# Norm hand-overs between layers, token half by token half, with the first two matmul units of each later norm laid tokens-on-partitions

## The reference

```python
for l in range(2):                                   # layers 0 and 1
    h = rmsnorm(x, g[0])
    y = even_mixer(h, ...) if l == 0 else odd_mixer(h, ...)
    x = x + rmsnorm(y, g[1])
    h = rmsnorm(x, g[2])
    x = x + rmsnorm(square(relu(h @ w1)) @ w2, g[3])
# then one hybrid layer:
h = rmsnorm_2(x, norm_g) * (1 + scale) + shift
proj = h @ w_in      # q, k, v, gates, convolution inputs
...
return rmsnorm_2(x + gate * (merged @ w_out), final_g)
```

## Time and profile before

| | us |
|---|---|
| median of 3 runs | 1006.33 |
| lowest and highest | 1002.78, 1007.84 |
| the profiled execution | 1001.67 |
| its span in the trace | 999.8 |
| PE busy | 972.2 (97%) |
| DVE busy | 646.5 (65%) |
| ACT busy | 503.0 (50%) |

### The profile page before, as it was taken

The page is one execution under the profiler, slowest core; times in us unless marked ns, Lnnn a source line. Parts: engine busy times, 40 slices in busy tenths (PEclk is TensorE's granted clock), DMA queues, the critical chain, the costliest instruction groups (busy, mean ns, idle before and its releaser), DMA issues.

```text
span 999.8 us, 14613 instructions
## 1 busy us (share of the span) xinstructions
PE 972.2 (97%) x6122; PEld 881.9 (88%) x6122; DVE 646.5 (65%) x821; ACT 503.0 (50%) x588; POOL 14.0 (1%) x12
## 2 busy tenths in 40 slices
PE   6999999999999999999999999998999999999997
PEld 5998888799999988888799999987989999988885
DVE  5889936567666658856567666657443777646473
ACT  6734464545444446565645444446444555435433
POOL 0000000000000000000000000000000000002000
PEclk9999999999999999999999999999999999999999
DMA  9834426457777773444457777791756445557511
GB/s 316 298 127 130 165 87 208 147 169 252 253 234 231 239 219 123 166 167 126 148 169 252 252 235 232 247 245 64 263 172 206 157 141 168 169 174 247 191 62 42
DMA packets 124900, 187.37 MB, mean 187 GB/s; under 512 B 5315, under 2 KB 92836, under 8 KB 124836
## 3 DMA queue, kind: packets, MB, share of 16 engines
q1 hardware_dynamic: 124676, 186.17, 57.3%
q10 hardware_dynamic: 160, 0.27, 0.1%
HBM read 185.37 MB, written 1.06 MB: 186 GB/s over the span
## 4 chain that ended last, share of the span: by engine, by line
PE 93%; DVE 4%; issue 1%; DMA 1%; ACT 1%; SPq 0%; DVEq 0%; ACTq 0%
PE bank L568 91%; DVE wl L982 1%; DVE scr L982 1%; DMA raw<-in_ev_w_in 1%; PE bank L724 1%; DVE arena L982 1%; PE bank L795 0%; DVE x L988 0%; DVE hl L988 0%; ACT wh L1515 0%; PE bank L869 0%; ACT arena L1510 0%; PE bank L683 0%; ACT hh L1510 0%; DVE work L985 0%
## 5 line engine op out<-in xcount | busy, mean ns | idle before, releaser
L982 DVE TENSOR_TENSOR wl<-raw,wh 128x2048 fp32r<-128x2048 f32 x156 | 356.3, 2289 | 212.1 <-ACT wh L1515 144.6
L1515 ACT CAST wh<-raw 128x2048 fp32r<-128x2048 f32 x156 | 295.4, 1905 | 166.1 <-PE bank L568 160.6
L568 PE MATMUL bank<-hh,wh 128*128 128x256 f32 x1152 | 319.0, 288 | 2.2 <-DVE wl L982 1.2
L568 PE MATMUL bank<-hh,wl 128*128 128x256 f32 x1152 | 313.8, 284 | 0.0
L568 PE MATMUL bank<-hl,wh 128*128 128x256 f32 x1152 | 304.5, 284 | 0.0
L568 PEld LDWEIGHTS bank<-hh,wh 128*128 128x128 f32 x1152 | 217.0, 194 | 3.3 <-issue 1.5
L568 PEld LDWEIGHTS bank<-hh,wl 128*128 128x128 f32 x1152 | 216.0, 192 | 0.2 <-DVE wl L982 0.2
L568 PEld LDWEIGHTS bank<-hl,wh 128*128 128x128 f32 x1152 | 212.4, 193 | 0.2
L568 PE MATMUL bank<-wh,yh 128*128 128x512 f32 x416 | 162.4, 390 | 0.0
L568 PE MATMUL bank<-wl,yh 128*128 128x512 f32 x416 | 162.0, 389 | 0.0
L568 PE MATMUL bank<-wh,yl 128*128 128x512 f32 x416 | 161.9, 389 | 0.0
(11 more groups left out here) (176 smaller groups left out, 705.1 us busy)
## 6 DMA issues: line engine op xcount, KB each, us to landing
raw<-in_mlp_w SPq DMA_DIRECT2D x64, 1024.0 KB, 5.7
raw<-in_w_in SPq DMA_DIRECT2D x40, 1024.0 KB, 5.1
raw<-in_ev_w_in SPq DMA_DIRECT2D x20, 1024.0 KB, 6.0
raw<-in_w_ada SPq DMA_DIRECT2D x12, 1024.0 KB, 5.2
raw<-in_od_w_in SPq DMA_DIRECT2D x12, 1024.0 KB, 5.2
raw<-in_ev_w_out SPq DMA_DIRECT2D x6, 1024.0 KB, 4.9
raw<-in_od_w_out SPq DMA_DIRECT2D x4, 1024.0 KB, 4.8
raw<-in_w_o_conv SPq DMA_DIRECT2D x4, 1024.0 KB, 4.9
```

The costliest lines, as they stand in the source:

```text
L568: return eng.matmul(o, l, r, start=start, stop=stop, skip_group_check=True)
L982: return eng.tensor_tensor(o, x, y, op)
L1515: eng.copy(part(wh, u), part(raw, u)).then_inc(S["hi"], 1)
```

## The change

The first two units of each later norm become T units. The two MLPs get a new role `uw0`, `uw1` for them (the first 512 hidden columns), whose result is then turned by 8 transposes (`hidden_turn`) so that the output projection finds features on partitions. In the mLSTM the first two `mv` units come ahead of `mqk`, in the hybrid layer the first two `av` units ahead of `aq`; the gates of the mLSTM move one or two units earlier or later with this. `t_first` takes the place of `a_first` and works token half by token half. `x_turn` is now called for one half: for the LATE norms the first half is turned inside `b_end`, ahead of the last 6 products of `y`'s last bank, and the second half inside `t_first`. ACT and DVE walk through one list, `hand_over`, with `hh` and `hl` in pieces of 128 x 128, the new `x` of the second half between pieces of the first half, and the split of unit `u+2` between the halves. `work` for the gates is now `hh + hl`.

```diff
     mlp(us, 0)
+    wide("od_w_in", 1024, 512, "mv")
     us.extend(("F", "od_w_in", 0, UCOLS * QK_ORDER[i], "mqk", i) for i in range(4))
-    wide("od_w_in", 1024, 1024, "mv")
+    wide("od_w_in", 1024, 1024, "mv", 2)
     wide("od_w_in", 2048, 1024, "mog")
     rows("od_w_out", 1024, "out2")
     mlp(us, 1)
+    wide("w_in", 2048, 512, "av")
     cols("w_in", 0, 1024, "aq")
     cols("w_in", 1024, 1024, "ak")
-    wide("w_in", 2048, 1024, "av")
+    wide("w_in", 2048, 1024, "av", 2)
     cols("w_in", 3072, 1024, "ag")
...
-        if j < 8:
+        if j == 0:
+            us.extend(("T", f"mlp_w1_{layer}", 512 * i, 0, f"uw{layer}", i) for i in range(2))
+        elif j < 8:
             us.extend(("F", f"mlp_w1_{layer}", 0, 512 * j + UCOLS * i, f"up{layer}", 2 * j + i) for i in range(2))
...
+            def t_first(u, n):
+
+
+                if n not in LATE:
+                    x_turn(n, 0)
+                for t in range(TT):
+                    dst = PS[t][:, :]
+                    wait_bank(eng, u, t)
...
+                        v = u + k // 4
+                        if t == 0 and k % 4 == 0:
+                            eng.wait_ge(S["hi"], SPLIT_OF[v] + 1)
+                            wait_low(eng, v)
+                        eng.wait_ge(S["hh"], h_count(n, t, k))
+                        mm(dst, hh[:, k, tokens(t)], slot(wh, v)[:, k % 4, :], k == 0, False)
+                        mm(dst, hh[:, k, tokens(t)], slot(wl, v)[:, k % 4, :], False, False)
...
+                        if (t, k) == (0, 4):
+                            x_turn(n, 1)
+                        v = u + k // 4
+                        eng.wait_ge(S["hl"], h_count(n, t, k))
+                        m = mm(dst, hl[:, k, tokens(t)], slot(wh, v)[:, k % 4, :], False, k == KT - 1)
+                        if (t, k) == (1, 3):
+                            m.then_inc(S["used"], 1)
+                    m.then_inc(S["t0"] if t == 0 else S["used"], 1)
+                if n in LATE:
+                    x_spread(n)
+
+            def hidden_turn(layer):
...
+            def hidden_turn(layer):
+
+                eng.wait_ge(S["sq"], 16 * layer + 2)
+                for i in range(2):
+                    for g in range(2):
+                        for t in range(TT):
+                            c = 512 * t + P * (2 * i + g)
+                            m = eng.transpose(hidden_turned(i)[:, g * SEQ + t * P:g * SEQ + (t + 1) * P], wf[:, c:c + P], ident[:, :])
+                    m.then_inc(S["hturn"], 1)
...
                             m.then_inc(S["used"], 1)
+                            if GROUP_AT.get(u + 1) in LATE:
+                                x_turn(GROUP_AT[u + 1], 0)
                         m = b_part(u, t, half, False, True)
...
-                        eng.wait_ge(S["yl_dve"], (p // 2) * 16 + i + 1)
+                        eng.wait_ge(S["yl_dve"], (p // 2) * 16 + max(i + 1, 2))
...
+            def hand_over(n, u):
+
+                p = n - 1
+                eng.wait_ge(S["d_grow"], 16 * n)
+                y_gain(p, 0, 0)
+                x_new(p, 0, y_gain(p, 0, 1))
+                y_gain(p, 1, 0)
+                if n in LATE:
+                    h_low(n, 0, 0)
+                    x_new(p, 1, y_gain(p, 1, 1))
+                    h_low(n, 0, 1)
+                    x_root(n, 0).then_inc(S["x_rs"], 1)
+                else:
+                    x_scaled(n, 0)
+                    x_new(p, 1, y_gain(p, 1, 1))
+                    h_low(n, 0, 0)
+                    x_scaled(n, 1)
+                    h_low(n, 0, 1)
+                split(u + 2)
+                h_low(n, 1, 0)
+                h_low(n, 1, 1)
+                if n in LATE:
+                    x_root(n, 1).then_inc(S["x_rs"], 1)
+                if n == 2:
+                    eng.wait_ge(S["hl"], h_count(n, 1, KT - 1))
+                    tt(work[:, :, :], hh[:, :, :].bitcast(F32), hl[:, :, :].bitcast(F32), ALU.add).then_inc(S["wk"], 1)
...
+            def hand_over(n, u):
+
+                p = n - 1
+                y_squares(p, 0, 0)
+                y_squares(p, 0, 1)
+                y_squares(p, 1, 0)
+                if n in LATE:
+                    h_high(n, 0)
+                    y_squares(p, 1, 1)
+                    eng.wait_ge(S["x_n"], x_count(n, 0, 1))
+                    x_root(n, 0)
+                    high(u + 2)
+                    h_high(n, 1)
+                    eng.wait_ge(S["x_n"], x_count(n, 1, 1))
+                    x_root(n, 1)
+                else:
+                    eng.wait_ge(S["x_n"], x_count(n, 0, 1))
+                    x_root(n, 0)
+                    y_squares(p, 1, 1)
+                    h_high(n, 0)
+                    eng.wait_ge(S["x_n"], x_count(n, 1, 1))
+                    x_root(n, 1)
+                    high(u + 2)
+                    h_high(n, 1)
...
+                if role in ("up0", "up1") and i == 3:
+                    hidden_turn_low(0 if role == "up0" else 1, 0)
+                    hidden_turn_low(0 if role == "up0" else 1, 1)
...
+                if u == at("mv", 3):
+                    ml_probs(0)
+                    ml_probs(1)
```

More of the change, by code:

```diff
@@ L568, in mm, with a_first, both @@
                 return eng.matmul(o, l, r, start=start, stop=stop, skip_group_check=True)
-            def a_first(u, norm):
-                units = (u,) if norm == 0 else (u, u + 1)
-                def both(v, w, h, k, first=False, last=False):
+            def a_first(u):
+                def both(w, h, k, first=False, last=False):
                     for g in range(2):
-                        m = mm(bank(v)[:, g * SEQ:(g + 1) * SEQ], w[:, k, g * P:(g + 1) * P], h[:, k, :], first and g == 0, last)
+                        m = mm(bank(u)[:, g * SEQ:(g + 1) * SEQ], w[:, k, g * P:(g + 1) * P], h[:, k, :], first and g == 0, last)
@@ L578, in both @@
                     return m
-                def low_products(v):
-                    for k in range(KT):
-                        eng.wait_ge(S["hl"], KT * norm + k + 1)
-                        m = both(v, slot(wh, v), hl, k, last=norm != 0 and k == KT - 1)
-                    return m
-                for v in units:
-                    if v != u:
-                        eng.wait_ge(S["hi"], SPLIT_OF[v] + 1)
-                    wait_bank(eng, v, BANK_OF[v])
-                    if norm != 0:
-                        wait_low(eng, v)
-                    for k in range(KT):
-                        eng.wait_ge(S["hh"], KT * norm + k + 1)
-                        both(v, slot(wh, v), hh, k, first=k == 0)
-                        if norm != 0:
-                            both(v, slot(wl, v), hh, k)
@@ L597, in a_first @@
-                if norm == 0:
-                    low_products(u)
-                    wait_low(eng, u)
-                    for k in range(KT):
-                        m = both(u, slot(wl, u), hh, k, last=k == KT - 1)
-                    m.then_inc(S["used"], 1)
-                    return
-                if norm in LATE:
-                    x_spread(norm)
-                for v in units:
-                    low_products(v).then_inc(S["used"], 1)
+                for k in range(KT):
+                    eng.wait_ge(S["hh"], k + 1)
+                    both(slot(wh, u), hh, k, first=k == 0)
@@ L920, in _ @@
                         b_forward(u)
+                if role in ("up0", "up1") and i == 2:
+                    hidden_turn(0 if role == "up0" else 1)
                 for j in items_of(u):
@@ new lines, in prenorm_first, with y_squares @@
+                    act(hh[:, k, :], x_bank(k), ACT.Copy, scale=col1[:, R_NORM + k:R_NORM + k + 1]).then_inc(S["hh"], 1)
+                high(1)
+            def y_squares(p, t, half):
+                wait_acc(eng, p, t, half)
+                squares(junk_y[:, 2 * t + half, :], acc(t, half)[:, :], 2 * t + half, S["ysq"])
+                if half == 0:
+                    eng.wait_ge(S["ysq"], 4 * p + 2 * t + 1)
+                    act(st[:, 8 + t:9 + t], st[:, 2 * t:2 * t + 1], ACT.Identity, scale=1.0 / D,
+                        bias=eps[:, 0:1]).then_inc(S["yb"], 1)
+                else:
+                    eng.wait_ge(S["ysq"], 4 * p + 2 * t + 2)
+                    eng.wait_ge(S["yb"], 2 * p + t + 1)
```

373 lines of the change are left out of this document (196 added, 177 removed).

## The result

The changed kernel takes 997.37 us (median; 995.88 to 998.85), the kernel before in the same runs 1006.27 (1002.78 to 1007.84). The ratio is 0.9915, 95% interval 0.9898 to 0.9932: 8.9 us less at the median, where 4.2 were forecast. The sign was as predicted, and so was the order of events at the hand-overs and in the MLPs. The size was not, and the two profiled executions hide why: they differ by only 5.8 us (1001.67 to 995.88 us; spans 999.8 and 994.0), and each is the fastest that its kernel showed up to here.

A forecast was written before the change was run, and what follows sets the result against it. PE, with 93% of the chain, sets the time and idles at the four hand-overs. MLPs -1.6, mLSTM -0.5, norm 4 -2.3 make -4.4, taken as -4.2: 1002.1 us from 1006.33; eight times in ten 997.0 to 1006.5.

The forecast's parts named there:

- The median of the runs stands 4.66 above it, so I forecast 1006.33 - 4.2: Final sum: the gain of 4.2 us against the profiled execution was subtracted unchanged from the median, giving 1002.1 us.
- so I leave this term at 0: mLSTM gate products: the clock fall after them, costing PE 1.7 us, was taken to remain, so no gain was counted.
- 1.7 more are gained: mLSTM: extra gain in us if the clock fall misses the new order, not fully additive to the wait there.
- rival (C): Clock falls around the moved transposes, 1.7 us each; gain gone from three, 1012.3 us with all six; chance 0.10.
- the wait that was to cost 1.6 us: mLSTM: PE waits for the first `ms` at `ml_scores(2)`, DVE's 28.2 us against PE's 26.6; bounds 0 and 3.
- Late hand-overs, -2.1 each: Norms 1 to 3: PE idles nowhere, each hand-over costs only 1.75 us of transposes instead of 3.8.
- The MLPs, -0.8 each: Both MLPs: -2.1 hand-over, -0.6 faster units, +0.9 `hidden_turn`, +1.0 wait for low parts.
- the wait for `yl`: First unit of `out1` and `out3`: PE waits for DVE's low parts, taken as 1.0 us, bounds 0 and 2.
- The mLSTM, -0.5: Norm 2: -2.1 from the hand-over, +1.6 from PE's wait for the first `ms`; no gain in pace.
- Norm 4, -2.3: Norm 4: group ends at 694.9 instead of 697.8, less 0.6 given back; two `hl` waits of 1.3 and 0.9.
- Rival (A): DVE keeps up everywhere, no waits in MLPs or mLSTM, low parts in time at norm 4: 996.0 us; chance 0.22 with middle.
- (B): Gap stays at the hand-overs, idle 1.7 us only moves to the second half: about 1007.2 us, no change; chance 0.13.

The follow-up runs named there:

- b_look1: Kernel before, unchanged, profiled again; b_look1 to 3 are three such profiles on one chip: 1006.27, 1007.21 and 1005.99 us.
- a_late: Changed kernel with the first-half transposes at norms 1 to 3 put back behind the previous phase's last products: 999.56 us, ratio to before 0.9939.
- a_low: Changed kernel with the MLPs' low parts of the turned hidden units ahead of the split and modulation rows in DVE's list: 995.13 us, ratio to before 0.9897.
- a_lp: a_low with DVE's first two probability products also put ahead of the split at the last value unit: 995.43 us, ratio to before 0.9891.
- b_fill: Kernel before with identity transposes, results overwritten, in PE's idle gaps at all four later norms: 1002.87 us, ratio to before 0.9974.
- b_fg: b_fill with the mLSTM's gate products and running-maximum products also spread: 1000.25 us, ratio to before 0.9951.
- a_g: Changed kernel with only the mLSTM's gate and running-maximum products spread: 996.37 us, ratio to before 0.9911.
- a_again: Changed kernel unedited, measured again in five rounds with a second profile: 997.68 us, ratio to before 0.9921.
- b_again: Kernel before, unchanged, measured and profiled again: 1006.16 us median, ratio to before 0.9992.
- a_lpg: a_lp with the mLSTM's gate and running-maximum products also spread: 992.70 us, ratio to before 0.9869.
- a_lpg2: a_lpg measured and profiled once more, on the chip of a_best: 992.46 us, ratio to before 0.9873.
- a_best: a_lpg with norm 4's third-unit split behind the second half's low parts and its high products moved earlier: 991.75 us, ratio to before 0.9869.

## Why the prediction was wrong, step by step

**The step that failed** is the one at the end: "The median of the runs stands 4.66 above it, so I forecast 1006.33 - 4.2". It carries the profiled execution's difference over to the median as if the 4.66 us were there before and after alike. They were not. They are three more falls of the clock (b_look1: five, the profile shown: two), two of them in the mLSTM and one behind norm 3's gap. With it belongs the sentence "so I leave this term at 0", said of the falls at the mLSTM's small products. The sum put the clock at nothing; a gain by it stands only in the sentence after ("1.7 more are gained"), without a chance, and rival (C) has it in the other direction.

What the runs showed in its place: with the clock out of the comparison the change is worth 4.0 us, as summed. The rest of the 8.9, 4 to 5 us, is the clock. The fall behind norm 3's gap is gone with the gap (1.5 us, in four of five profiles). In the mLSTM the usual execution before has two or three falls, and the changed kernel one and two in its two profiles (a_late one, a_low none, a_lp three); the wait that was to cost 1.6 us is hidden where one stands at the first scores. Why they come less often after the change, while the gate products stand there in one piece as before, stays open.

By ratios, each against runs of before on its own chip, and of 1006 us: filling the gaps is worth 2.6 us (b_fill), spreading the small products another 2.3 (b_fg), together 4.9 us of clock in the kernel before. The steps of the change at full clock are worth 4.0 (b_fg to a_g). Of the clock's share the changed kernel leaves 1.0 (a_g to a_again; the falls in the mLSTM, whose cost is partly the wait that they cover). 4.9 + 4.0 - 1.0 = 7.9 us, which is a_again's ratio; 8.9 in the first set of runs is the same within the error.

- *Late hand-overs, -2.1 each*: right. At norms 1 to 3 PE idles nowhere. From the start of the hand-over to the next F unit it takes 12.95 us after (192.40 to 205.35) and took 15.84 before (192.48 to 208.32): -2.9 where -2.7 was said. The pieces of 128 columns take 0.28 us (four in 1.12, against 0.26 taken), those with scale and bias 0.34 (0.36). The fixed part of an instruction was thus sized well enough, though the two rows used, 0.40 and 0.70 us, give 0.10 and not 0.13 for it. That small instructions pay it is what the Trainium skill ("VectorE: DVE Perf Modes", section on the TRN2 errata) says; halving the pieces paid nonetheless, as DVE keeps ahead of PE here.
- *The MLPs, -0.8 each*: right, -0.9 in every pair of profiles. `hidden_turn` costs 0.79 us (0.9), the wait for `yl` 0.90 in the trace and 1.0 to 1.1 with a_low's stage as measure (1.0).
- *The mLSTM, -0.5*: right at full clock, -0.68 from b_fg to a_g with a wait of 1.28 us (1.6). DVE's chain, counted at 28.2 us from the end of `mqk` unit 1, took 28.2 in the profile after, from 406.13 to the end of the first `ms` at 434.38. But in both profiles of the changed kernel the clock falls at the first scores, PE comes later by as much as it would have waited, and the stage gains 2.15 with the same two falls on both sides (b_again to a_again), 3.7 from b_look1 to 3. "PE waits 1.6 us" holds only if PE is at full clock, and the prediction didn't say so. This is the second term that was mis-sized, by 1.6 to 3.2 us. The fall's price, 1.7 us in the prediction, is 1.3 to 1.5.
- *Norm 4, -2.3*: somewhat too much. -1.7 from b_fg to a_g, -2.1 in the first pair, where a fall in the gap of before makes 0.3 of it. The waits came as counted, 1.23 and 0.62 us for 1.3 and 0.9.
- *Rival (A)*, 996.0, was closest in time and wrong in mechanism: the waits of DVE that it denied are there. That 997.37 lies inside the span given for eight times in ten, at the end that stood for (A), is therefore luck. *(B)* did not happen. *(C)* had the sign of the clock's part reversed: in the nine profiles with the change no transpose between products is followed by a fall. The Trainium skill ("TensorE: Matmul & The Clock Gate", Part 4) says that transposes don't count as busy for the clock in the same way as products. b_fill's norm 4, 3.65 us of nothing but transposes at a granted clock of 1.00, where idling went with a fall in six of six profiles, doesn't bear that out for this kernel's f32 transposes; the trace lists them as MATMUL and doesn't tell whether they are what that page means.

## What to carry over

One profile is one execution. Where its time stands away from the median, as here 4.7 us, find what the difference is made of (a second and third profile, the list of stretches at half clock) before a sum made against it is carried to the median. An idle gap of PE costs its length and, with a frequency that only several profiles show, a stretch at half clock behind it (here never at norms 1 and 2, mostly at norm 3, always at norm 4); a run of very small products was followed by one too. Spread the small products between large ones. And a wait counted from lists holds for the clock it was counted at: a slower PE hides it, a kernel freed of falls brings it out.

## What the runs showed of the hardware

- Transposes of a 128x128 f32 identity, their results overwritten, put into idle time, made the kernel before 0.26% faster by the ratio (medians 1002.87 and 1005.92 us).
- The same program shows two to five stretches of 3.4 us at half clock between 20 us and its last 5 us. Which gaps they follow is not even: never norm 1 or 2 in five profiles, norm 3 in four of five, norm 4 in five of five, with the same 1.7 us of idling at the first three. Why the gaps at norms 1 and 2 go free was not tried.
- In 64 executions of that program the time goes with the mean granted clock, 0.87 us more for each 0.001 less of it.
- At a run of 16 small products of 8 columns (3.6 us at full clock, PE shown as busy all the time) a fall comes in ten of twelve profiles that have it in one piece, behind the run or, in b_look1, inside it; spread over two places, in none of five.
- With the falls gone, the runs of a kernel lie closer together: within 0.3, 0.7 and 0.4 us for a_g, a_lpg and a_lpg2 (four runs each), 1.4 and 2.5 for a_best and b_fg (four and five), against 2.6 to 5.3 us in the sets of four to six runs of the other kernels with the change.
